# A hybrid RWKV / attention / SSM block on one core: the order of the weight splits, the sigmoids and the scan's preparation in the first mixer

## The reference

```python
hn = rmsnorm(h, g[0])
y = hn @ w_in                                  # [528, 1024] @ [1024, 2304]
ys = ys + (prev - ys) * mu                     # token shift
r, k, v, wd, ad, gd = split(ys)
decay = exp(-exp(wlog)),  wlog = -softplus(-(w0 + tanh(wd) @ w_up)) - 0.5
a = sigmoid(a0 + ad @ a_up);  g = sigmoid(gd) @ g_up
kk = k * k_k / max(norm(k * k_k), 1e-12);  k = k * (1 + (a - 1) * k_a)
S = S * w_t + (S @ -kk_t) (kk_t * a_t) + v_t k_t;  o = S r_t      # 528 steps
```

## Time and profile before

| | before |
|---|---|
| median of 3 runs | 2656.52 us |
| the profiled execution | 2656.52 us, span 2654.7 us |
| PE busy | 2417.0 us (91%) |
| PEld busy | 1720.0 us (65%) |
| DVE busy | 1400.5 us (53%) |
| ACT busy | 1042.4 us (39%) |
| POOL busy | 440.0 us (17%) |

### The profile page before, as it was taken

One profiled execution on the slowest core, in us unless ns is written; L12 is line 12 of the kernel. 1 busy time (PEld: TensorE's weight loads), 2 busy tenths in 40 slices (PEclk: granted clock), 3 DMA queues, 4 the chain that ended last, 5 costly groups with the idle time before them and its releaser, 6 DMA issues. The chain is left out here.

```text
span 2654.7 us, 41623 instructions
## 1 busy us (share of the span) xinstructions
PE 2417.0 (91%) x16643; PEld 1720.0 (65%) x16652; DVE 1400.5 (53%) x2209; ACT 1042.4 (39%) x1805; POOL 440.0 (17%) x526
## 2 busy tenths in 40 slices
PE   7999989999979989689999999879889998899998
PEld 6888768888856666366444775546555887744445
DVE  6675366522553444456533376553542545498733
ACT  6345342322333343243332346246552454443322
POOL 0375430012330000150001411015240000000000
PEclk9999799999989987689999999888878999999999
DMA  4211013222210101012223122010011240122222
GB/s 154 81 56 43 1 67 125 96 96 96 83 48 25 48 32 64 1 67 96 96 96 122 69 96 95 18 56 12 29 55 54 84 170 21 64 96 107 96 88 76
DMA packets 38937, 190.95 MB, mean 72 GB/s; under 512 B 12176, under 2 KB 14608, under 8 KB 17624
## 3 DMA queue, kind: packets, MB, share of 16 engines
q1 hardware_dynamic: 37944, 186.08, 19.6%
q10 hardware_dynamic: 800, 2.20, 0.3%
HBM read 185.08 MB, written 3.19 MB: 71 GB/s over the span
## 5 line engine op out<-in xcount | busy, mean ns | idle before, releaser
L454 DVE SCALAR_TENSOR_TENSOR wsp<-raw_w,wsp 128x2048 f16<-128x2048 f32 (+2 forms) x180 | 400.1, 2223 | 202.8 <-ACT wsp L434 197.9
L417 PE MATMUL ps<-hn,wsp 128*128 128x512 f16 x1968 | 432.5, 381 | 6.9 <-DVEq L241 4.8
L412 PE MATMUL ps<-hn,wsp 128*128 128x256 f16 (+1 forms) x2976 | 356.9, 283 | 46.1 <-DVEq L241 15.1
L434 ACT ACTIVATE wsp<-raw_w 128x2048 f16<-128x2048 f32 (+2 forms) x180 | 326.8, 1816 | 114.2 <-PE ps L415 48.2
L412 PEld LDWEIGHTS ps<-hn,wsp 128*128 128x128 f16 x2976 | 298.7, 102 | 101.7 <-POOL hn L892 16.7
L417 PE MATMUL ps<-big,wsp 128*128 128x512 f16 (+1 forms) x1740 | 351.4, 364 | 7.3 <-DVEq L241 7.3
L417 PEld LDWEIGHTS ps<-hn,wsp 128*128 128x128 f16 x1968 | 192.6, 98 | 236.3 <-DVEq L241 5.3
L415 PE MATMUL ps<-hn,wsp 128*128 128x264 f16 x2880 | 340.6, 282 | 3.6 <-DVE hn L718 3.6
L415 PEld LDWEIGHTS ps<-hn,wsp 128*128 128x128 f16 x2880 | 287.3, 100 | 52.8 <-issue 4.4
L417 PEld LDWEIGHTS ps<-big,wsp 128*128 128x128 f16 x1740 | 174.1, 101 | 174.9 <-issue 22.9
L412 PE MATMUL ps<-big,wsp 128*128 128x256 f16 (+1 forms) x1800 | 205.2, 276 | 1.3 <-ACT big L467 0.7
(11 more groups left out here) (409 smaller groups left out, 3028.2 us busy)
## 6 DMA issues: line engine op xcount, KB each, us to landing
raw_w<-slabs SPq DMA_DIRECT2D x162, 1024.0 KB, 5.1
raw_w<-slabs SPq DMA_DIRECT2D x10, 512.0 KB, 5.5
raw_w<-slabs SPq DMA_DIRECT2D x8, 384.0 KB, 5.0
h<-xin SPq DMA_DIRECT2D x2, 1056.0 KB, 7.1
out<-hn SPq DMA_DIRECT2D x8, 256.0 KB, 2.3
big<-memx ACTq DMA_DIRECT2D x1, 1024.0 KB, 5.1
sml<-small SPq DMA_DIRECT2D x1, 768.0 KB, 14.4
cst<-consts SPq DMA_DIRECT2D x1, 582.0 KB, 13.1
```

The costliest lines, as they stand in the source:

```text
L412: mm = L.eng.matmul(ps[:rows, b, 0:T // 2], lhsT, rhs[:, z, :], start=first, stop=last)
L417: mm = L.eng.matmul(two(ps[:rows, b, 0:T]), lhsT, rhs, start=first, stop=last)
L434: L.fin(L.eng.activation(wsp[:, n % NW, 0, lo:hi], raw_w[:, q % 2, 0:hi - lo], ACT.Copy, scale=WSCALE), "hi")
L454: L.fin(L.eng.scalar_tensor_tensor(wsp[:, n % NW, 1, lo:hi], raw_w[:, q % 2, 0:hi - lo], WSCALE, wsp[:, n % NW, 0, lo:hi], ALU.mult, ALU.s ...
```

## The change

Five moves, with the arithmetic the same. (1) DVE: the sums of squares go ahead of the memsets; the memsets of `steps` go behind the reciprocal; the low half of slab 0 is made in two places, its second part now between the scaling of tile 1 and tile 2; slab 1's low half goes ahead of the first two token shifts. (2) ACT: slab 0's high half is made wholly behind the root, and the square of the keys of p = 2 goes ahead of the four sigmoids L2200. (3) DVE: `key_decay` is merged into `key_norm`, head pair by head pair. (4) ACT: slab 3's high half goes ahead of the copies of the Grams. (5) POOL: `widened(0)`, with its wait for DVE's second "elem", goes ahead of the meta tokens' inverse.

```diff
@@ first_squares_act
-            split_hi_part(L, cnt)
             root_act(L, cnt, T0)
-            split_hi_part(L, cnt)
@@ scale_dve(..., split_at=None)
             for j in range(nt + 1):
+                if j == split_at:
+                    split_lo_part(L, dcnt)
@@ ACT
             first_squares_act(L, cnt)
+            split_hi(L, cnt)
             scale_act(L, n1, DT, T0)
...
-                if p == 2:
-                    for j in range(4):
-                        evac(... X[0][:, j, :] ... ACT.Sigmoid, bias=V("ev_w0", j)))
                 if 1 <= p < 5:
...
                     L.fin(act.activation(sq[:, (p - 1) % 2, :], y(p + 3), ACT.Square, ...), "kks")
                 if p == 2:
+                    for j in range(4):
+                        evac(... X[0][:, j, :] ... ACT.Sigmoid, bias=V("ev_w0", j)))
...
-                if p in (3, 11):
+                if p in (3, 7, 11):
                     split_hi(L, cnt)
...
                         L.tell("nst")
-                    split_hi(L, cnt)
@@ DVE
+            first_sums_dve(L)
             L.step(dve.memset(yv[:, :, 0:1], 0.0))
+            dcnt["square"] = DT - 1
+            rms_dve(L, dcnt, T0, nt=0, keep=True, part=0)
+            split_lo_part(L, dcnt)
+            dve.wait_ge(sem("in_r"), 16)
             L.step(dve.memset(steps, 1.0))
...
-            split_lo_part(L, dcnt)
-            rms_dve(L, dcnt, T0, nt=0, keep=True, part=0)
-            split_lo_part(L, dcnt)
...
-            scale_dve(L, n1, h1, DT, T0, lambda j: V("norm_g", j), "hn")
+            scale_dve(L, n1, h1, DT, T0, lambda j: V("norm_g", j), "hn", split_at=2)
+            split_lo(L, dcnt)
...
                 if p == 6:
                     for j in range(4):
                         key_norm(j)
-                    for j in range(4):
-                        key_decay(j)
                     L.tell("elem")
                 shift_mix(p, sc[:, 0, :])
-                if p == 1:
-                    split_lo(L, dcnt)
@@ POOL
+            pool.wait_ge(sem("elem"), 2)
+            widened(0)
             pool.wait_ge(sem("moved"), 160)
...
             L.tell("inv0")
-            pool.wait_ge(sem("elem"), 2)
-            widened(0)
```

More of the change, by code:

```diff
@@ L707, in times_rinv, with scale_dve @@
             return L.eng.scalar_tensor_tensor(halves(t, T), halves(src, T), gain, bank(6, T), ALU.mult, ALU.mult)
-        def scale_dve(L, dst, src, nt, T, gain, tell):
+        def scale_dve(L, dst, src, nt, T, gain, tell, split_at=None):
             for j in range(nt + 1):
+                if j == split_at:
+                    split_lo_part(L, dcnt)
                 if j < nt:
@@ L2197, in _ @@
                     L.fin(act.activation(yv[0:64, 12, 1:YW], yv[0:64, 12, 1:YW], ACT.Tanh), "tg")
-                if p == 2:
-                    for j in range(4):
-                        evac(L, cnt, T0, lambda v: act.activation(halves(X[0][:, j, :], T0), v, ACT.Sigmoid,
-                                                                  bias=V("ev_w0", j)))
                 if 1 <= p < 5:
@@ L2208, in _ @@
                     for j in range(4):
+                        evac(L, cnt, T0, lambda v: act.activation(halves(X[0][:, j, :], T0), v, ACT.Sigmoid,
+                                                                  bias=V("ev_w0", j)))
+                    for j in range(4):
                         evac(L, cnt, T0, lambda v: act.activation(halves(X[2][:, j, :], T0), v, ACT.Sigmoid,
@@ L2759, in _ @@
             L.step(dve.memset(steps[:, META:T0:CH], 0.0))
-            first_sums_dve(L)
-            dcnt["square"] = DT - 1
-            split_lo_part(L, dcnt)
-            rms_dve(L, dcnt, T0, nt=0, keep=True, part=0)
-            split_lo_part(L, dcnt)
-            dve.wait_ge(sem("in_r"), 16)
             L.step(ts(nkk, par[:, COL["ev_k_k"]:COL["ev_k_k"] + 4], -1.0, None, ALU.mult))
@@ L2781, in key_norm @@
                 L.take("st_full")
-                k = KA[:, j, :]
+                k, e = KA[:, j, :], X[1][:, j, :]
                 L.fin(stt_(halves(k, T0), halves(y(4 + j), T0), nkk[:, j:j + 1], bank(6, T0), ALU.mult, ALU.mult),
@@ L2785, in key_norm @@
                 L.step(tt(X[2][:, j, :], X[2][:, j, :], k, ALU.mult))
-            def key_decay(j):
-                k, e = KA[:, j, :], X[1][:, j, :]
                 L.step(tt(k[:, 1:META], k[:, 1:META], e[:, 0:META - 1], ALU.mult))
```

## The result

| | before | after |
|---|---|---|
| median (11 runs each) | 2655.63 us | 2671.20 us (2666.78 to 2678.36) |
| ratio, 95% interval | | 1.0062 (1.0047 to 1.0078) |
| profiled execution, span | 2656.52, 2654.7 us | 2669.14, 2667.4 us |
| PE busy | 2417.0 us | 2423.1 us |
| first L415 | 23.65 | 26.65 |

The changed kernel is slower by 15.6 us, 0.6%. The forecast was slower by 10.2 us (2666.7). The direction and the places were right, the size was too small: on the forecast's own base of 2656.52 the ratio gives 2673.0, just above its range of 2657 to 2672. The profiled execution itself lost 12.7 us of span. It lost 14.9 by the first L1588, and some 3 came back behind L1674.

What follows compares the result with a forecast made beforehand. PE, busy 91% of the span, was taken as the bound. PE's lateness of 8.0 us at tile 3's end plus 2.2 us at the scan's start gave +10.2 us on 2656.52: 2666.7 us, range 2657 to 2672.

Steps and rivals of the forecast that it cites:

- The start: Behind tile 2, PE's fourth small unit starts at 51.9 instead of 45.62, +6.3 us, from low halves, memsets and the square's move.
- The clock: Small units behind tile 2: PE's clock falls at about 52.1, adding 1.7 us; PE is 8.0 us late at tile 3's end.
- The prediction's upper bound: PE's lateness at tile 3's end if the clock stays low further into tile 3: +9.6 us.
- The head pairs: PE's pitch goes from 2.57 to 3.26 us through DVE's contention with POOL: +1.4 us for PE at tile 7.
- The inverses: Scan's start: POOL, held to DVE's pace, delivers the meta inverse late, so L1571 comes +2.2 us beyond the late start.
- the sum: 8.0 us at tile 3's end plus 2.2 us at the scan's start: +10.2 us, giving 2666.7 us.
- The clock holds: Rival: PE's clock does not fall in the small units behind tile 2; 3.4 + 2.2 = +5.6 us, 2662; chance 0.19.
- Longer on both counts: Rival: clock low into tile 3 (+9.6) and +3.0 at the inverses; +12.6 us, 2669; chance 0.12.
- POOL is not held: Rival: POOL runs free of DVE and its meta inverse is in time; 8.0 - 0.6 = +7.4 us, 2664; chance 0.13.
- The Grams decide: Rival: the scan's release hangs on Grams, inversion and spread inverse, 3.05 us earlier, a gain: 2653.5; chance 0.08.

Runs made afterwards that it cites:

- the filler at L1571: All five moves plus twelve unused dense float16 products of 512 columns on PE ahead of its wait in the scan's first chunk: 2662.9 us, 1.0025.
- the fillers: All five moves plus unused dense float16 products on PE, ahead of its first and fourth small units (2658.0 us) or also ahead of L1571 (2661.0 us).
- the profile with both: All five moves plus unused dense products: six ahead of PE's first small unit, thirteen ahead of the fourth, twelve ahead of L1571: median 2661.0 us, 1.0018.
- the start's: All five moves plus unused dense float16 products on PE, six ahead of its first small unit and thirteen ahead of the fourth: 2658.0 us, 1.0013.
- both halves ahead: Kernel before with move 4, and ACT making both parts of slab 0's high half ahead of the root: 2654.2 us, 0.9993.

## Why the prediction was wrong in size

- **The start** was right: 26.65, 35.92, 46.3 for the end of the tanh, 52.23 for the fourth unit (forecast 26.7, 35.9, 46.05, 51.9). Of the shift of 6.6 us there, undoing move 2 took back 1.7, and 2.5 at tile 3's end (forecast 2.2).
- **The clock** is the step that failed: "The clock fell 6.6 us after the dense matmuls ended. If it does so again, it falls at about 52.1", and behind it tile 3 "takes its 6.57 again". It fell at 47.8, 2.8 us after tile 2's end at 44.99 and behind an idle stretch of PE of 1.42 us, and it stayed low for 20.5 us, nearly through tile 3. From forecast to measured the pieces are: fourth unit starts 0.3 later and runs 0.5 longer, column sum 0.55, four units 0.3, tile 3 1.3 longer. Together 3.0 us: tile 3 ended 10.97 us late, not 8.0. The prediction's upper bound was 9.6.
- **The moment of the fall is only half of it.** Six profiled kernels have the same instructions up to tile 3 (all five moves twice, without move 3, without move 5, moves 1 and 2 alone, the filler at L1571). Their clock fell at 46.8 to 48.8 in five, and at 52.9, as forecast, in the one without move 5. There tile 3 still ended at 70.26, 9.9 us late, because the clock stayed low until 66.6. The forecast lets it be low for some 12 us (52.1 until 2.1 us into tile 3, an estimate from the kernel before); measured were 13.7 to 20.5. Dense products at this place moved the fall to 55.1 and 56.7, later than in any of the six, and tile 3's end to 68.64 and 67.04. Whether the idle time or the small units make it fall is not separated, since the products take the place of the one and stand between the others. In kernels whose PE idled only 0.35 us there it fell too, 6.2 to 7.0 us behind tile 2.
- **The head pairs** were right: pitch 3.26, PE at tile 7 another 1.39 us late (12.36 against 10.97). The Trainium skill, "GPSIMD Engine Reference", section "Key points", on the shared SBUF interfaces, agrees with it: 0.97 or 0.98 us beside POOL's L3018 in each of four pairs, and with move 3 undone the pitch was 2.56 again.
- **The inverses** were right in kind and size: L1571 1.85 us late beyond tile 3 (forecast 2.2), POOL's steps one for one beside DVE's (0.30 every 0.37 us beside the inversion, 0.74 beside the token shifts). The Grams left at 114.10, 0.8 us later than forecast: their low half took 5.42 us instead of 4.62. The read-back took 7.6 us from L1788 to L3048 instead of 8.75, and the two nearly cancel.
- **What was missing** is a second fall, at the scan's start: a term that the sum put at nothing. With 3.01 us of idle PE at L1571, the instructions up to L1588 cost 2.06 us more, and in the repeated execution the rest of the scan another 7.0. The two experiments that take the wait or its idleness away, without move 5 and with the filler, both keep the clock and are 7 to 8 us faster in the median.
- **That the wait makes the clock fall is likely, but not shown.** All seven profiles with a wait of 0.99 to 3.69 us at L1571 have a fall there. Of the nine whose wait is absent or filled, three have one, move 4 alone for 10.2 us. And in three of the seven (without move 1, 2 or 3) the clock fell within 0.1 us of the wait's start, too early for its idle time to have brought it about; there the wait can at most have made the stretch longer.
- **The rivals.** "The clock holds" was wrong for this kernel. It is what the fillers come near to, and the medians with them (2658 and 2661) lie about the 2662 that it gave, though the profile with both has L1571 12.6 us late, not 5.6. "Longer on both counts" was the nearest in time (2669) and only half right: longer at the clock, not at the inverses. "POOL is not held" is out: POOL's last step ended at 167.92, beside DVE's last token shift at 167.84. "The Grams decide" is out for this kernel; where the start isn't late, move 4 lets PE start the scan's operands without its 2.00 us wait, and L1571 came up to 3.1 us earlier.

The sum as the runs have it: 10.97 + 1.85 + 2.06 = 14.9 us at the first L1588, and 15.6 in the medians. The span lost only 12.7; behind L1674 the profile after is 3.1 us quicker, with 315.3 us at the low clock there for 321.7. Open stays why medians move by more than the profiles up to the scan show (8 us for the filler at L1571, whose L1588 stands 0.3 us earlier; 13 for the start's). The time at the low clock behind L1674 was between 301 and 322 us in the sixteen profiles; it can move a time by several us, and no run separates it from the rest. So the 14.9 us of one profile have their causes in its rows, and the share of each fall in the medians is not shown.

## What to carry to other kernels

Price a wait on TensorE twice: its length, and what the engine does around it at half the clock. Here a wait of 3 us went with 5 us in one profile, and its removal or filling with 7 to 8 us in the medians. Where such a wait can't be avoided, dense products that nobody reads kept the clock at 1.00 in the scan in all three profiles that had them at its start, though four of them ahead of the fourth unit did not move the fall there (48.6); where no wait was left they cost their own 2.6 us. A gain or loss of a few us needs many runs of each kernel, since one profile's clock differs from the next. And before work moves from behind a wait to ahead of it on a side engine, ask which result is due first: POOL's was.

## What the runs showed of the hardware

- The granted clock's fall does not follow from the work alone. After the same instructions it stayed low for 6.8 us in one execution of the changed kernel's scan and for 20.5 us in another. In the kernel with both halves ahead PE idled less ahead of L1571 than in the kernel before (1.19 against 2.00 and 1.19 us), and the clock fell there and not before; with move 4 alone it fell for 10.2 us behind 1.19 us of idle time. Over six profiles with the same instructions up to tile 3 it fell first at 46.8 to 52.9 us and stayed low for 13.7 to 20.5.
- A PE that is busy throughout with small float32 products can run at half the clock (7.00 of 7.00 us busy at 0.51 in the earlier trace rows, 10.00 of 10.00 at 0.51 in the scan of move 4 alone); with dense float16 products among them it was as busy, 3.00 of 3.00, at 1.00. The Trainium skill, "TensorE: Matmul & The Clock Gate", section "What's actually happening", has a throttled default that activity releases; the rows with the fillers agree, the one of the earlier trace rows only half.
- Four copies of 64 x 64 on POOL took 5.32 us beside two of DVE's 128 x 2112 products, and 1.11 us in the kernel before, at 151.30, where DVE did other work.
